# Last attention of a two-block transformer kernel as flat steps of both heads

## The reference

```python
s_c = jnp.einsum('bqgid,bngd->bqgin', qc, k_cmp) * scale      # compressed keys: 31 blocks
p_c = masked_softmax(s_c, m_c)
o_c = jnp.einsum('bqgin,bngd->bqgid', p_c.astype(v_cmp.dtype), v_cmp)
...
s_s = jnp.einsum('bqgid,bqgnld->bqginl', qr, kg) * scale      # selected blocks
...
s_w = jnp.einsum('bqgid,bkgd->bqgik', qr, kw) * scale         # window of 512
...
return g[..., 0:1] * o_c + g[..., 1:2] * o_s + g[..., 2:3] * o_w
...
y = o.reshape(B, S, ATTN_D) * jax.nn.silu(z)
return x + y @ w_out
```

## Time and profile before

| | |
|---|---|
| median of three runs | 2420.7 us |
| the profiled execution: time, span of the core | 2415.6 us, 2413.8 us |
| TensorE busy over the span | 2273.4 us, 94% |
| VectorE, ScalarE, GpSimd busy | 1298.2 us (54%), 921.1 us (38%), 250.7 us (10%) |
| this attention | from about 2036 to 2352 us of the span |

### The profile page before, as it was taken

How to read it: one execution, slowest core, us unless ns; L and a number is a source line. 1 busy time by engine, 2 the same in 40 slices (tenths; PEclk the granted TensorE clock), 3 DMA queues, 4 the chain that set the end, 5 groups by cost and what they waited for, 6 DMA issues and landing times.

```text
span 2413.8 us, 34422 instructions
## 1 busy us (share of the span) xinstructions
PE 2273.4 (94%) x10882; PEld 1855.7 (77%) x10882; DVE 1298.2 (54%) x2537; ACT 921.1 (38%) x1850; POOL 250.7 (10%) x143
## 2 busy tenths in 40 slices
PE   7986999999999799999999999999999689999997
PEld 6675777888888687788888888888887667777766
DVE  5876444666644566466664454555544643545443
ACT  4433453322322266432223332222223334555551
POOL 0042221000001111110000210000002000011112
PEclk8998999999999999999999999999999889999888
DMA  3121111332333110223232332222222312000001
GB/s 131 51 88 53 61 53 62 96 101 90 104 102 102 66 36 26 77 90 99 93 104 96 104 97 96 99 99 96 96 96 79 113 63 85 2 19 9 19 10 70
DMA packets 50053, 182.93 MB, mean 76 GB/s; under 512 B 5552, under 2 KB 5680, under 8 KB 49840
## 3 DMA queue, kind: packets, MB, share of 16 engines
q1 hardware_dynamic: 49824, 181.35, 22.9%
q0 software_dynamic: 144, 0.52, 0.1%
HBM read 179.76 MB, written 2.10 MB: 75 GB/s over the span
## 4 chain that ended last, share of the span: by engine, by line
PE 83%; DVE 7%; issue 4%; ACT 3%; POOL 1%; DMA 1%; DVEq 0%; ACTq 0%; POOLq 0%; SPq 0%
PE pj L1863 68%; PE ps L2006 4%; PE po L2062 4%; PE pt L2022 2%; ACT w_hi L670 1%; DMA raw<-in_wstream 1%; PE po L2047 1%; PE ps L2176 1%; DVE s_sb L1303 1%; PE pj L1973 1%; DVE rtmp L1248 1%; DVE w_lo L1118 1%; PE po L2071 1%; ACT p_sb L757 1%; DVE rtmp L1245 1%
## 5 line engine op out<-in xcount | busy, mean ns | idle before, releaser
L1863 PE MATMUL pj<-h_hi,w_hi 128*128 128x512 f32 x1736 | 706.9, 407 | 21.0 <-DVE w_lo L1118 15.6
L670 ACT ACTIVATE w_hi<-raw 128x1024 fp32r<-128x1024 f32 x334 | 353.7, 1059 | 865.6 <-PE pj L1863 848.8
L1863 PE MATMUL pj<-h_lo,w_hi 128*128 128x512 f32 x1736 | 683.8, 394 | 0.0
L1863 PE MATMUL pj<-h_hi,w_lo 128*128 128x512 f32 x1736 | 683.6, 394 | 0.0
L1118 DVE TENSOR_TENSOR w_lo<-raw,w_hi 128x1024 fp32r<-128x1024 f32 x288 | 390.4, 1356 | 392.2 <-ACT w_hi L670 391.9
L1863 PEld LDWEIGHTS pj<-h_hi,w_hi 128*128 128x128 f32 x1736 | 331.1, 191 | 90.1 <-issue 17.1
L1863 PEld LDWEIGHTS pj<-h_hi,w_lo 128*128 128x128 f32 x1736 | 330.5, 190 | 71.1
L1863 PEld LDWEIGHTS pj<-h_lo,w_hi 128*128 128x128 f32 x1736 | 331.5, 191 | 64.6 <-issue 1.4
L1863 PE MATMUL pj<-G_hi,w_hi 128*128 128x512 f32 x704 | 278.1, 395 | 3.1 <-DVE G_lo L1367 3.0
L1863 PE MATMUL pj<-G_lo,w_hi 128*128 128x512 f32 x704 | 276.0, 392 | 0.0
L1863 PE MATMUL pj<-G_hi,w_lo 128*128 128x512 f32 x704 | 275.9, 392 | 0.0
(11 more groups left out here) (295 smaller groups left out, 2531.4 us busy)
## 6 DMA issues: line engine op xcount, KB each, us to landing
raw<-in_wstream SPq DMA_DIRECT2D x334, 512.0 KB, 3.4
xT<-in_x SPq DMA_DIRECT2D x4, 512.0 KB, 9.5
out_x<-xT SPq DMA_DIRECT2D x4, 512.0 KB, 2.7
memT<-in_mem SPq DMA_DIRECT2D x1, 1024.0 KB, 12.3
...
```

Source lines behind the costliest of these rows:

```text
L670: nc.scalar.activation(w_hi[:, c.par * CW:(c.par + 1) * CW], raw[:, c.par * CW:(c.par + 1) * CW], ACT.Copy).then_inc(hi_ready, 1)
L1863: mm = nc.tensor.matmul(acc, w[:, col:col + P], x[part], start=first and k == 0, stop=last and k == 2)
```

## The change

The attention `nq` gets code of its own (`Sweep`, and `sweep_...` on each engine). A tile is now nine steps: four of `slc` (b = 0 to 3), four of `win`, and one of `cmp`, the last; a step takes both heads. All 72 steps stand one after the other without a loop.

- Scores: one matmul per head over 64 partitions (the head's own rows of `qs` and of the keys, which lie in `n_k` once, with no zeros), head 0 into `ps0`, head 1 into `ps1`. TensorE does the scores of step s+2, the transposes of s, the values of s-1, then its eighth of the projection (in the first eight steps of tiles 0 to 5).
- VectorE takes the row minimum of the negated and scaled scores in one instruction with the mask, so that the separate scaling goes. The masked scores lie in three buffers in turn (`slots`), and the exponential overwrites them.
- `cmp`: four score matmuls of 32 columns per head, one mask addition per head, one maximum over groups, one subtraction and one exponential for all eight units; one transpose per head; one value matmul per head with 128 rows and 256 columns against a block-diagonal `cmp_v`, which is built with zeros beforehand (stage `cmp2`: a wider copy and three more small copies on ScalarE).
- ScalarE copies both heads' transposes at once where they are at most 256 wide.
- GpSimd has nothing left to do in this attention. Its additions of the branches, the low part of the output and the low parts of the weight chunks go to VectorE. Its clearing of 2 x 4096 columns of `n_k` becomes one of 1024 columns of `cmp_v`.

```diff
--- before.py
+++ after.py
...
+        self.steps = [("slc", b) for b in range(NB)] + [("win", b) for b in range(NB)] + [("cmp", 0)]
+        self.n, self.ends = len(self.steps), (NB - 1, 2 * NB - 1, 2 * NB)
...
-            nc.gpsimd.memset(n_k["win"][:, :], 0.0)
-            nc.gpsimd.memset(n_k["slc"][:, :], 0.0).then_inc(zeroed, 1)
...
-            def branch_sum(i, j, p):
-                t = i * 2 + j
-                pool.wait_ge(om_ready, t * 2 + p)
-                pool.wait_ge(o_scaled, ATT["nq"].first_pass + t * 3 + p)
-                settle(pool)
-                nc.gpsimd.tensor_tensor(o_sb[:, :], o_sb[:, :], om[:, :], ALU.add).then_inc(o_scaled, 1)
...
+            nc.gpsimd.memset(cmp_v[:, :], 0.0).then_inc(zeroed, 1)
...
+            def sweep_exp(s):
+                t, k, p, branch, b, w = NSA.at(s)
+                slot = slots[s % 3]
+                if branch == "cmp":
+                    act.wait_ge(step_max, 2 * s + 2)
+                    nc.scalar.activation(pc[:, :], slot[:, 0:2 * P], ACT.Exp, scale=NSA.scale).then_inc(step_exp, 2)
+                    return
+                for hh in range(2):
+                    r = p * 8 + b * 2 + hh
+                    here = slot[:, hh * S:hh * S + w]
+                    act.wait_ge(step_max, 2 * s + hh + 1)
+                    nc.scalar.activation(here, here, ACT.Exp, scale=-1.0, bias=ST(s % 3, hh),
+                                         accum_out=lsum[:, r:r + 1]).then_inc(step_exp, 1)
+            def sweep_copy(s):
+                w = NSA.at(s)[5]
+                dst = turned[s % 2]
+                if s > 1:
+                    act.wait_ge(step_valued, s - 1)
+                if w <= MEM:
+                    act.wait_ge(step_turned, 2 * s + 2)
+                    nc.scalar.activation(dst[:, 0:2 * w], pt[s % 2][:, 0:2 * w], ACT.Copy).then_inc(step_copied, 2)
+                    return
+                for hh in range(2):
+                    act.wait_ge(step_turned, 2 * s + hh + 1)
+                    nc.scalar.activation(dst[:, hh * S:hh * S + w], pt[hh][:, 0:w], ACT.Copy).then_inc(step_copied, 1)
...
+                for s in range(NSA.all + 5):
+                    t, k = divmod(s, NSA.n)
+                    if s + 1 < NSA.all:
+                        sweep_exp(s + 1)
+                    if s < NSA.all:
+                        sweep_copy(s)
+                    if k == 0 and t < NSA.tiles - 1:
+                        split_hi(At(CH["nq"] + t + 3))
+                    if k == 4 and t:
+                        gated_hi(t - 1)
...
+            def sweep_max(s):
+                t, k, p, branch, b, w = NSA.at(s)
+                slot = slots[s % 3]
+                if s >= 3:
+                    dve.wait_ge(step_turned, 2 * s - 4)
+                if branch == "cmp":
+                    dve.wait_ge(step_scored, 2 * s + 2)
+                    for hh in range(2):
+                        nc.vector.tensor_tensor(slot[:, hh * P:(hh + 1) * P], ps[hh][:, 0:P],
+                                                C("cmp", 0, P), ALU.add).then_inc(step_taken, 1)
+                    dve.wait_ge(step_taken, 2 * t + 2)
+                    each = slot[:, 0:2 * P].rearrange("p (u n) -> p u n", u=8)
+                    link(nc.vector.tensor_reduce(cmx[:, :], each, mybir.AxisListType.X, ALU.max))
+                    nc.vector.tensor_tensor(each, each, cmx[:, :].unsqueeze(2).broadcast_to([P, 8, NCMP]),
+                                            ALU.subtract).then_inc(step_max, 2)
+                    return
+                for hh in range(2):
+                    dve.wait_ge(step_scored, 2 * s + hh + 1)
+                    nc.vector.tensor_tensor_reduce(out=slot[:, hh * S:hh * S + w], in0=ps[hh][:, 0:w],
+                                                   in1=causal(b), scale=-NSA.scale, scalar=3.0e38, op0=ALU.add,
+                                                   op1=ALU.min, accum_out=ST(s % 3, hh)).then_inc(step_max, 1)
...
+            def sweep_pass(t, p):
+                c = sweep_sums(t, p)
+                dve.wait_ge(step_valued, t * NSA.n + NSA.ends[p] + 1)
+                if p == 0:
+                    dve.wait_ge(o_turned, NSA.first_tile + t)
+                dst = om if p else o_sb
+                part = nc.vector.tensor_tensor(dst[:, :].rearrange("p (r c) -> p r c", r=8),
+                                               po[(t * 3 + p) % 2][:, :].rearrange("p (r c) -> p r c", r=8),
+                                               c.unsqueeze(2).broadcast_to([P, 8, 64]), ALU.mult)
+                if p:
+                    part.then_inc(om_ready, 1)
+                    dve.wait_ge(om_ready, t * 2 + p)
+                    part = nc.vector.tensor_tensor(o_sb[:, :], o_sb[:, :], om[:, :], ALU.add)
+                part.then_inc(o_scaled, 1)
...
+                split_lo(At(CH["nq"] + 2))
+                sweep_max(0)
+                sweep_max(1)
+                for s in range(NSA.all + 6):
+                    t, k = divmod(s, NSA.n)
+                    if s + 2 < NSA.all:
+                        sweep_max(s + 2)
+                    if k == 0 and t:
+                        sweep_pass(t - 1, 1)
+                    if k == 1 and t:
+                        sweep_pass(t - 1, 2)
+                    if k == 3 and t:
+                        gated(t - 1)
+                    if k == 5 and t < NSA.tiles:
+                        sweep_pass(t, 0)
+                    if k == 5 and t:
+                        gated_lo(t - 1)
+                    if k in (4, 6) and t < NSA.tiles - 1:
+                        query(NSA, 0, t + 1, k // 2 - 2)
+                    if k == 7 and t < NSA.tiles - 1:
+                        split_lo(At(CH["nq"] + t + 3))
+                    if k == 8 and t < NSA.tiles - 2:
+                        take_query(NSA, 0, t + 2)
...
+            def sweep_scores(s):
+                t, k, p, branch, b, w = NSA.at(s)
+                g, par = t // 2, t % 2
+                if k == 0:
+                    pe.wait_ge(roped, RP["nq"] + t + 2)
+                for hh in range(2):
+                    rows = slice(hh * 64, hh * 64 + 64)
+                    if s and k == 0:
+                        pe.wait_ge(step_taken, 2 * t - 1 + hh)
+                    elif s:
+                        pe.wait_ge(step_max, 2 * s - 1 + hh)
+                    if branch == "cmp":
+                        for c in range(NB):
+                            mm = nc.tensor.matmul(ps[hh][:, c * NCMP:(c + 1) * NCMP],
+                                                  qn[rows, par * S + c * P:par * S + (c + 1) * P],
+                                                  cmp_k[rows, g * NCMP:(g + 1) * NCMP], start=True, stop=True)
+                    else:
+                        mm = nc.tensor.matmul(ps[hh][:, 0:w], qs[rows, par * S + b * P:par * S + (b + 1) * P],
+                                              n_k[branch][rows, g * S:g * S + w], start=True, stop=True)
+                    mm.then_inc(step_scored, 1)
+            def sweep_turn(s):
+                t, k, p, branch, b, w = NSA.at(s)
+                last = NSA.last_in_turned(s)
+                if last is not None:
+                    pe.wait_ge(step_copied, 2 * last + 2)
+                for hh in range(2):
+                    pe.wait_ge(step_exp, 2 * s + hh + 1)
+                    src = pc[:, hh * P:(hh + 1) * P] if branch == "cmp" else slots[s % 3][:, hh * S:hh * S + w]
+                    bank_, first = NSA.turned_columns(s)[hh]
+                    for kb in range(w // P):
+                        mm = nc.tensor.transpose(pt[bank_][:, first + kb * P:first + (kb + 1) * P],
+                                                 src[:, kb * P:(kb + 1) * P], ident)
+                    mm.then_inc(step_turned, 1)
+            def sweep_values(s):
+                t, k, p, branch, b, w = NSA.at(s)
+                g, src, acc = t // 2, turned[s % 2], po[(t * 3 + p) % 2]
+                if b == 0 and p == 0 and t:
+                    pe.wait_ge(om_ready, t * 2 - 1)
+                if b == 0 and p == 1 and t:
+                    pe.wait_ge(y_ready, t)
+                if p == 2:
+                    pe.wait_ge(o_scaled, NSA.first_pass + t * 3 + 1)
+                pe.wait_ge(step_copied, 2 * s + 2)
+                for hh in range(2):
+                    if branch == "cmp":
+                        mm = nc.tensor.matmul(acc[:, :].rearrange("p (b h c) -> p h b c", b=NB, h=2)[:, hh],
+                                              src[:, hh * P:(hh + 1) * P],
+                                              cmp_v[:, g * NB * 64:(g + 1) * NB * 64].rearrange("p (b c) -> p b c", b=NB),
+                                              start=True, stop=True)
+                        continue
+                    r = b * 2 + hh
+                    first = hh * w if w <= MEM else hh * S
+                    for kb in range(w // P):
```

(18 more changed lines are left out.)

225 lines of the change are left out of this document (107 added, 118 removed).

## The result

The changed kernel takes 2338.4 us (median of 4 runs, 2335.1 to 2349.9), the kernel before 2418.7: a ratio of 0.967, 95% interval [0.965, 0.970]. I had forecast 2367, with 2350 to 2402 as the range.

The account below looks back on a forecast made before the run. TensorE bounds the attention. Tiles of 249.6 us, with start and end 255.0, plus 11 for low clock give 266 against 316.2; 50.2 less than 2415.6 is 2365.4, named 2367, range 2350 to 2402.

Parts of the forecast that it names:

- I take this middle value: Two heads' scores on TensorE: overlap gains a quarter, 2.2 us a tile, between bounds of nothing and 4.4; chance 0.45.
- Changes of form: TensorE going into and out of 64-row scores nine times a tile: 0.23 us each, 2.1 us a tile.
- idle time: TensorE standing idle in the attention: 1.5 us a tile with projection, 3.0 without.
- The clock lost: Low clock in the attention: 11 us instead of 31.6, 7 at the start and 4 in the two last tiles.
- TensorE's border: TensorE's work in a tile's first two steps: 5.0 to 5.6 us, against 6.5 us on VectorE.
- the tile at a mean of 0.81: Kernel before, a tile with projection: 43.9 us, against 37.0 at full clock, 6.9 lost.
- The tile of before from its parts: TensorE's work in a tile of the kernel before: sum 34.2 us, 28.7 without projection.
- The condition that stages ahead must not move by over 2 us: Sign of being wrong: stages ahead of 2036 us, where the attention begins, move by over 2 us.
- The first, no overlap at 2385: Rival: the two heads' scores on TensorE don't overlap, 17.6 us lost, 2385 and up to 2400; chance 0.34.
- The second: Rival: the clock falls at every tile's border, 52 us more, 2419 with overlap, 2437 without; chance 0.12.
- The third, full overlap at 2352: Rival: the array's halves overlap fully on both heads' scores, 17.6 us more gained, less some at borders; chance 0.09.
- the 3.4 that the prediction put on the compressed branch: Compressed branch on TensorE: 2.9 us a tile instead of 6.3, a gain of 3.4.

Follow-up runs that it names:

- same_half: Changed kernel with both heads' scores of the last attention on the same upper 64 rows of the array; 2405.8 us, ratio 0.995 to before.
- heads_apart: Changed kernel with the second head's scores issued after the step's transposes, not right behind the first head's; 2524.5 us, ratio 1.044 to before.
- full_rows: Changed kernel with each score using all 128 rows, so both heads' products are summed; 2350.5 us, ratio 0.971 to before.
- before_flat: Kernel before with only the last attention's loop over tiles written out; 2405.4 us, ratio 0.994 to before.
- one_ahead: Changed kernel with each step's scores issued one step ahead on TensorE instead of two; 2380.3 us, ratio 0.984 to before.

## Why the prediction was wrong

**The step that failed** is "I take this middle value": that the two heads' scores overlap by a quarter. They overlap fully, 4.51 us a tile instead of 2.2. I had given this 0.09, because the queue holds head 0's two records before head 1's two. The Trainium skill's TensorEngine Tiling (Array Packing), Key Properties, says that tiles of the array load weights and multiply in parallel; the trace agrees, 1.06 against 1.91 us. Its other property, that a change of form drains TensorE, agrees too: 0.10 in and 0.19 out.

**The sizes, step by step**, for the attention. At full clock I had 255.0 us; measured are 242.1 - 7.3 = 234.8. The next two terms are eight times a middle tile's. Overlap: 8 x 2.31 = 18.5 less. Changes of form: 2.69 a tile and not 2.1, so 4.7 more. What is left, 6.4 less, is mostly idle time, an estimate: 0.57 us in a middle tile and not 1.5. The split is rough: over the whole attention same_half at full clock (0.87 x 302.5 = 263.1) is 28.3 us longer than the changed kernel, not 8 x 4.51 = 36. By that the overlap is worth 11 us more than forecast, not 18.5, and 14 are left. A part of the gap comes from the rule itself, which takes a low stretch as all work, though idle time doesn't grow with the clock (same_half's tile of 43.49 us at 0.76 gives 33.1, where its full-clock tiles take 34.37). TensorE's idle time in the whole attention, from its row, is 242.1 - 230.7 = 11.4 us where the forecast had 20.4 (6 x 1.5 + 2 x 3.0 + 1.9 + 3.5): 9 less, between the two. The clock lost 7 us and not 11: 4 less. Together 24 less, and the output projection starts at 2274.7, not 2302. Outside, the attention began 3.6 us earlier and the stretch behind it was 0.7 shorter (60.7 us; 61.4). 2365.4 - 20.2 - 3.7 - 3.6 - 0.7 = 2337.2, and the profiled execution took 2337.1.

**Two slips in the prediction's working.** With the overlapped scores TensorE's border is 2.3 + 0.7 + 1.3 + 0.5 = 4.8 us, not 5.0. And the tile at a mean of 0.81 loses 0.19 x 43.9 = 8.3 us by the rule used for the whole attention, where the prediction put 6.9, the difference to a full-clock tile. Neither moves a term of the sum by which 2367 came out.

**What was right.** The tile of before from its parts, VectorE's load, the idle at the start (1.9; 2.0), the end, and that TensorE stays the bound. The condition that stages ahead must not move by over 2 us was too narrow: in the sixteen profiles of this study, with all but the same code ahead of it, the attention begins between 2030.8 and 2041.6 us.

**The rivals.** The first, no overlap at 2385, was wrong twice over: that case, same_half, takes 2406. Overlap and clock are not two independent terms, as I had them: without overlap one half works alone, and the clock falls. The second was wrong for the changed kernel, whose clock is at 0.97. I had tied the clock to idle time at the borders; a lone half brings it down with no idle time at all, and heads_apart, the same work in another order, is 4.4% slower than before. The third, full overlap at 2352, had the mechanism right and is still 14 us too slow, for the idle time and the clock that it shares with my forecast.

**Where the gain is.** full_rows, the change without its 64-row form, is at 0.971, so most of the 80 us comes from the flat steps. The attention takes 316.2 us before, 301.5 with the loop written out (before_flat), 250.1 with the steps in full rows (full_rows) and 242.1 with the two halves. Of the middle 51.4 us about 31 are in the tiles at full clock, 8 x (35.54 - 31.68), and most of the rest is clock: 24 us lost in before_flat, 0.01 x 250 = 2.5 in full_rows. The 3.86 us a tile are near the 3.4 that the prediction put on the compressed branch, but no run takes that form alone. one_ahead shows that two steps ahead are needed in the new order; it is no part of the gain, since the kernel before already did its scores three units ahead. The two halves bring 1.82 us a tile over full rows, 4.51 less 2.69, and 5 to 12 us in all, with intervals that overlap: the step on which the forecast failed is a small part of what the change gained.
